# A two-layer block and a three-branch block on one core: a place for each weights' unit inside a longer slot, and a ring with one slot less

## The chip, the cores and the metric

The kernel runs on one core of a Trainium2 chip. The metric is the device time of one execution in microseconds, lower is better. Everything is computed in 32-bit floating point as far as the reader of the output can see; inside, TensorE multiplies in fp32r, a 32-bit format of which the kernel makes two parts for each number (below).

## The reference, cut to what matters

A sequence of 256 tokens with 1024 features goes through two layers, an even one and an odd one, and then through a second block with another set of weights. Norms are RMS norms over 1024 features.

```python
for layer in range(2):                      # first_block
    y = rms_norm(h, nw[0])
    y = even_mixer(y, ...) if layer % 2 == 0 else odd_mixer(y, ...)
    h = h + rms_norm(y, nw[1])
    y = conv_ffn(rms_norm(h, nw[2]), ffn_w_up[layer], conv_w, conv_b, ffn_w_down[layer])
    h = h + rms_norm(y, nw[3])
# even_mixer: proj = y @ w_in; window attention with rope and sinks, beside a gated
#             recurrence in blocks of 32 tokens (HGRN2); concat @ w_out
# odd_mixer:  proj = y @ w_in; attention in chunks of 64 with a relative bias; @ w_out
# conv_ffn:   up = y @ w_up (1024 x 5632); gelu(conv3(u)) * v; @ w_down (2816 x 1024)
# second block: proj = y @ w_in_2; three attentions (block-sparse, with forget gates, over a
#             memory of 256 rows); each @ its branch matrix, gated and summed; @ w_out_2;
#             then a gated feed-forward of the same size as above
```

Nearly all of the arithmetic is in the products of 256 tokens with weights that are read once from memory.

## The kernel before

**Units and slots.** The weights come as 347 units, at most 128 partitions by 1024 numbers each, in the order in which TensorE uses them (`STREAM`: even_a, even_f, even_q, even_i, fill, even_out, lead0, up0, down0, odd_v, odd_qk, odd_out, lead1, up1, down1, moba_qk, both_v, fox_qk, mem_q, forget, gates, branches, merge_out, lead2, up2, down2). For each unit three things are kept in SBUF: the raw numbers, the high part (the raw numbers rounded to fp32r) and the low part (raw minus high). They stand in slots: `raw` and `hi` are tensors of `RAW` = 10 slots of 1024 numbers, and `lo` takes the same addresses as `raw`, since the split overwrites in place. `ring()` says which slot a unit takes and which earlier unit, its giver, must have been used before; up to the end of fill only `FEW` = 8 slots are in the ring, because the last two hold the memory's normed rows (`m_hi`, `m_lo`) until then.

**One unit's way.** SP issues the load (L500) after it has waited until TensorE has used the giver (`unit_used`). ACT waits for the load and rounds (L593, `round_unit`), DVE waits for ACT and subtracts (L1483, `split_unit`), and TensorE waits for DVE (`lo_done`). The orders of ACT's and DVE's work are written out by hand: a call `units(upto)` between other work says up to which unit they shall have gone on.

```python
act.activation(hi[:, s, :w], raw[:, s, :w], ACT.Copy).then_inc(hi_done, 1)
...
dve.tensor_tensor(lo[:, s, :w], raw[:, s, :w], hi[:, s, :w].bitcast(F32), ALU.subtract).then_inc(lo_done, 1)
```

**Three products.** The tokens are kept in a high and a low part as well (`y_hi` and `y_lo`, the two halves of `y_both`; `h_hi` and `h_lo` for the feed-forward's inner features). A product of tokens and weights is the sum of high by high, high by low and low by high. Where tokens are the stationary operand (`tokens_unit`, L927: even_a, odd_v, down, merge_out and others; the same pattern at L1142, L1157, L1190, L1283 and L1344), the moving operand is 512 or 256 columns of a weights' part. Where weights are stationary, the moving operand is the tokens: `features_of` (L1008) moves 256 columns three times, `features_pair` (L1017 and L1018, the units of up) moves `y_both`, 512 columns, against the high part and `y_hi`, 256 columns, against the low part.

**Changes of stage.** Before even_out, down, odd_out and merge_out end, the last `TAIL` = 7 units are gone through for the first tile of 128 tokens and then for the second (`by_tile`), so that the first tile's norm runs while TensorE works on the second. The next stage begins with `LEAD` = 6 units gone through in the same way. Between the two lies a norm (on ACT, DVE and POOL), the turning of the normed rows by TensorE (L1029, `turn`), and the making of y_hi on ACT and y_lo on DVE. `norms_between` on ACT, and a like function on DVE, say how many units are prepared between the parts of the norm:

```python
units(last(name) + RAW - TAIL)
square_product(g, 0, base, tile_done, TAILS.index(name) + 1)
square_sum(g + 1, 0, p)
units(last(name) + 4)
turned_hi(stage, turn_base, y_hi, (0,))
units(last(name) + 5)
```

`BIAS_AT`, the points in the stream at which SP loads the odd layer's bias, counts from `RAW` too.

Of the kernel before, what the change touches and what calls it, by code (L numbers as in the profile page):

```python
# [44 lines left out]
UNIT = 1024  # L45
RAW = 10

# [15 lines left out]
UNITS = len(WIDTH)  # L63
FEW = 8

# [22 lines left out]

SLOT, GIVER, TURN = ring()
TAILS = ["even_out", "down0", "odd_out", "down1", "merge_out", "down2"]  # L90

# [113 lines left out]
def build(nc, dram, out):  # L205
    with ExitStack() as ctx:
# [237 lines left out]
        def token_half(y, kh, t):  # L444

            return y[:, 4 * kh:4 * kh + 4, t * P:(t + 1) * P]

        @block.sync
        def _(sp):
# [463 lines left out]
        def _(pe):  # L913
# [3 lines left out]
            def tokens_unit(name, n, t, base, y, splits, lo_last=False, y_lo_at=None):  # L917

                yh, yl = y
                k, tok = n - FIRST[name], slice(t * P, (t + 1) * P)  # L920
                for i, (x, w) in enumerate(((yh, hi), (yl, hi), (yh, lo)) if lo_last else ((yh, hi), (yh, lo), (yl, hi))):
                    if i == 2 and lo_last:
# [3 lines left out]
                    for half_, (c0, cw) in enumerate(splits):  # L926
                        mm = pe.matmul(ps[:, base + 2 * t + half_, :cw], x[:, k, tok], w[:, SLOT[n], c0:c0 + cw],  # L927
                                       start=i == 0 and k == 0, stop=i == 2 and n == last(name) - 1)
                return mm

            def last_unit(y):

                n, k = UNITS - 1, COUNT["down2"] - 1
                for c in range(2):
                    for x, w in ((y[0], hi), (y[0], lo), (y[1], hi)):
                        mm = pe.matmul(ps[:, 6 + c, :], x[:, k, P:S], w[:, SLOT[n], 512 * c:512 * c + 512],
                                       start=False, stop=x is y[1])
# [57 lines left out]

            def features_of(n, s, outs, y, nk=KD, cols=P, stage=None):

# [4 lines left out]
                for f, dst in enumerate(outs):  # L1002
                    for k in range(nk):
                        if stage is not None and k % 4 == 0:
                            pe.wait_ge(y_lo_done, 4 * stage + 3 + k // 4)
                        at = slice(k * cols + f * P, k * cols + (f + 1) * P)
                        for w, x, first, final in ((hi, yh, True, False), (hi, yl, False, False), (lo, yh, False, True)):
                            mm = pe.matmul(dst, w[:, s, at], x(k), start=first and k == 0, stop=final and k == nk - 1)  # L1008
# [110 lines left out]
            for f in range(4):  # L1119
                n = FIRST["even_f"] + f  # L1120
                features_of(n, SLOT[n], [ps[:, f // 2, (f % 2) * S:(f % 2 + 1) * S]], of_tiles(Y)).then_inc(unit_used, 1)
            for f in range(4):
# [4 lines left out]
                n = FIRST["even_q"] + f  # L1127
                features_of(n, SLOT[n], [ps[:, 2 + f // 2, (f % 2) * S:(f % 2 + 1) * S]], of_tiles(Y)).then_inc(unit_used, 1)
            pe.wait_ge(qf_evac, 2)
# [6 lines left out]
            for n in range(FIRST["even_i"], last("even_i")):  # L1136
                wait_unit(n)
                for t in range(NT):
                    for kk in range(2):
                        k = 2 * (n - FIRST["even_i"]) + kk  # L1140
                        for x, w in ((y_hi, hi), (y_hi, lo), (y_lo, hi)):
                            mm = pe.matmul(ps[:, 4 + t, :], x[:, k, t * P:(t + 1) * P], w[:, SLOT[n], 512 * kk:512 * kk + 512],  # L1142
                                           start=k == 0 and x is y_hi and w is hi, stop=k == KD - 1 and x is y_lo)
                mm.then_inc(unit_used, 1)

            def fill(first, a, b):

                for i, k in ((first + step // KD, step % KD) for step in range(a, b)):
# [5 lines left out]
                    if t == 0 and k % 4 == 0:  # L1154
                        wait_unit(n)
                    for x, w in ((yh, hi), (yh, lo), (yl, hi)):
                        mm = pe.matmul(ps[:, 6, t * 256:t * 256 + 256], x[:, k, t * P:(t + 1) * P], w[:, SLOT[n], c],  # L1157
                                       start=k == 0 and x is yh and w is hi, stop=k == KD - 1 and x is yl)
                    if t == 1 and k % 4 == 3:
# [24 lines left out]
            def even_part(u, t):  # L1184
                n, k, tok = FIRST["even_out"] + u, (u + 4) % 8, slice(t * P, (t + 1) * P)
                if t == 0:
                    wait_unit(n)
                for x, w in ((y_hi, hi), (y_hi, lo), (y_lo, hi)):
                    for c in range(2):
                        mm = pe.matmul(ps[:, (0, 6)[t] + c, :], x[:, k, tok], w[:, SLOT[n], 512 * c:512 * c + 512],  # L1190
                                       start=u == 0 and x is y_hi and w is hi, stop=u == KD - 1 and x is y_lo)
                if t == 1:
# [65 lines left out]
            def feed_forward(layer, stage, base, turn_next=lambda: None):  # L1258
# [3 lines left out]
                def lead(t):  # L1262
                    tok = slice(t * P, (t + 1) * P)
                    for j in range(LEADS):
                        for half_ in range(2):
# [7 lines left out]
                            if j == 0:  # L1273
                                pe.wait_ge(y_hi_done, 4 * stage + 2 * t + half_ + 1)
                            order = ((y_hi, hi), (y_lo, hi), (y_hi, lo)) if last_lead else ((y_hi, hi), (y_hi, lo), (y_lo, hi))
                            for i, (x, w) in enumerate(order):
# [4 lines left out]
                                for kk in range(4):  # L1281
                                    k, c = 4 * half_ + kk, slice(256 * kk, 256 * kk + 256)
                                    mm = pe.matmul(lead_place(layer, j, t), x[:, k, tok], w[:, SLOT[n], c],  # L1283
                                                   start=k == 0 and i == 0, stop=k == KD - 1 and i == 2)
# [41 lines left out]
            def qk_half(j, f):  # L1326
# [3 lines left out]
                if j >= 2:  # L1330
                    pe.wait_ge((q_evac, k_evac)[f], j - 1)
                features_of(n, SLOT[n], [qk_place(j, f)], of_tiles(Y)).then_inc(unit_used, 1)

# [4 lines left out]
            def out_part(k, t):  # L1338
                n, tok = FIRST["odd_out"] + k, slice(t * P, (t + 1) * P)
                if t == 0:  # L1340
                    wait_unit(n)
                for x, w in ((0, hi), (0, lo), (1, hi)):
                    for c in range(2):
                        mm = pe.matmul(ps[:, (6, 0)[t] + c, :], out_y(x, k // 4, tok)[:, k % 4, :], w[:, SLOT[n], 512 * c:512 * c + 512],  # L1344
                                       start=k == 0 and x == 0 and w is hi, stop=k == KD - 1 and x == 1)
                if t == 1:
# [55 lines left out]
            def gate_unit(u):  # L1402
                if u >= 2:
                    pe.wait_ge(gate_evac, u - 1)
                for f in range(2):
                    n = FIRST["gates"] + 2 * u + f
                    features_of(n, SLOT[n], [ps[:, 6 + u % 2, f * S:(f + 1) * S]], of_tiles(Y)).then_inc(unit_used, 1)

            pe.wait_ge(v2_evac, 2)
            n = FIRST["forget"]  # L1410
            features_of(n, SLOT[n], [ps[:, 1, 0:S]], of_tiles(Y)).then_inc(unit_used, 1)
            pe.wait_ge(c_evac, 2)
# [42 lines left out]
            for u in range(6):  # L1455
# [11 lines left out]
                for i in range(2):  # L1467
                    n = FIRST["branches"] + 2 * u + i
                    outs = [ps[:, 2 * (u % 2) + i, f * S:(f + 1) * S] for f in range(2)]
                    features_of(n, SLOT[n], outs, ys, 4, 256).then_inc(unit_used, 1)  # L1470
            tokens_by("merge_out", 4, (h_hi, h_lo), needs=lambda u: (merged_lo, u // 4 + 1),
# [508 lines left out]
```

## Time and profile before

| what | value |
|---|---|
| median of 3 runs | 1099.36 us (1096.43 to 1099.52) |
| the profiled execution: its own time, and its span | 1095.97 us, 1094.2 us |
| TensorE busy with matmuls | 1086.5 us, 99%, 6712 instructions |
| weight loads | 959.7 us, 88% |
| DVE | 746.0 us, 68% |
| ACT | 600.1 us, 55% |
| POOL | 112.4 us, 10% |
| DMA | 192.81 MB, mean 176 GB/s; weights' queue 54.1% of 16 engines' span |

The span is that of the instructions on the core; the time has what lies around it as well. Matmuls are pipelined and overlap in the record, so the duration that a row gives for one of them is longer than the time from its start to the next one's start.

### The profile page before, as it was taken

To read this page: it belongs to the slowest core of one execution; us is meant where nothing else is said; L and a number is where in the kernel's file an instruction comes from. 1 tells how busy PE (TensorE), PEld (TensorE's weight loads), DVE (VectorE), ACT (ScalarE), POOL (GpSimd) and SP (SyncE) were. 2 spreads that over 40 slices of the span, in tenths; PEclk is the share of its full clock that TensorE was granted. 3 is DMA by queue.
4 is the path that set the end of the run, shared out by engine and by line. 5 is a ranking of instruction groups with operands and counts; after the bars stand their busy time and mean duration, and the time that the engine had idled before them with its cause. 6 is when DMAs were issued, how large, how long until landed. Compare 5 with 4: busy or idle time off the path is not lost.

```text
span 1094.2 us, 16724 instructions
## 1 busy us (share of the span) xinstructions
PE 1086.5 (99%) x6712; PEld 959.7 (88%) x6712; DVE 746.0 (68%) x1107; ACT 600.1 (55%) x994; POOL 112.4 (10%) x129
## 2 busy tenths in 40 slices
PE   8999999999999999999999999999999999999998
PEld 7988989888888899898888888889999989888887
DVE  6876595998846566859788566766656885666651
ACT  5744465776734545557667445357444644555640
POOL 5020000121100000001111001121000000111100
PEclk9999999999999999999999999999999999999999
DMA  8851366665664754366656656464333545565661
GB/s 304 286 174 59 121 206 213 193 189 190 182 193 152 269 150 149 124 225 188 188 190 183 194 183 211 136 234 134 115 99 113 165 160 196 190 182 185 191 194 39
DMA packets 56957, 192.81 MB, mean 176 GB/s; under 512 B 6704, under 2 KB 9648, under 8 KB 56880
## 3 DMA queue, kind: packets, MB, share of 16 engines
q1 hardware_dynamic: 56880, 191.74, 54.1%
q8 instruction: 53, 0.87, 0.3%
q14 instruction: 24, 0.20, 0.1%
HBM read 190.67 MB, written 1.05 MB: 175 GB/s over the span
## 4 chain that ended last, share of the span: by engine, by line
PE 94%; DVE 3%; POOL 1%; issue 1%; ACT 1%; DMA 0%; SPq 0%; DVEq 0%; ACTq 0%
PE ps L927 28%; PE ps L1017 19%; PE ps L1008 15%; PE ps L1018 10%; PE ps L1283 5%; PE ps L1157 3%; PE ps L1103 3%; PE ps L1080 2%; PE ps L1344 2%; DVE lo L1483 1%; PE ps L1092 1%; PE ps L1029 1%; PE ps L1142 1%; POOL hr L538 1%; PE ps L1049 1%; PE ps L1167 1%
## 5 line engine op out<-in xcount | busy, mean ns | idle before, releaser
L1483 DVE TENSOR_TENSOR lo<-raw,hi 128x1024 fp32r<-128x1024 f32 (+2 forms) x347 | 429.0, 1263 | 81.0 <-ACT hi L593 78.3
L593 ACT ACTIVATE hi<-raw 128x1024 fp32r<-128x1024 f32 (+2 forms) x347 | 347.3, 1037 | 84.3 <-DMA raw<-in_weights 77.6
L1017 PE MATMUL ps<-y_both,hi 128*128 128x512 f32 x912 | 320.8, 397 | 0.0
L1018 PE MATMUL ps<-y_both,lo 128*128 128x256 f32 x912 | 255.0, 280 | 0.0
L1017 PEld LDWEIGHTS ps<-y_both,hi 128*128 128x128 f32 x912 | 171.3, 188 | 41.5
L1018 PEld LDWEIGHTS ps<-y_both,lo 128*128 128x128 f32 x912 | 172.0, 189 | 0.0
L1008 PE MATMUL ps<-y_both,hi 128*128 128x256 f32 x912 | 167.6, 285 | 0.4 <-DVE lo L1483 0.4
L1008 PEld LDWEIGHTS ps<-y_both,hi 128*128 128x128 f32 x912 | 141.8, 191 | 1.1 <-DVE lo L1483 0.6
L1008 PE MATMUL ps<-y_both,lo 128*128 128x256 f32 x456 | 128.9, 283 | 0.0
L927 PE MATMUL ps<-hi,y_both 128*128 128x512 f32 x352 | 93.9, 381 | 1.1 <-DVE lo L1483 1.0
L927 PE MATMUL ps<-hi,h_hi 128*128 128x512 f32 x294 | 90.9, 391 | 0.0
L927 PE MATMUL ps<-lo,h_hi 128*128 128x512 f32 x294 | 90.6, 389 | 0.0
L927 PE MATMUL ps<-hi,h_lo 128*128 128x512 f32 x294 | 90.6, 389 | 0.0
L1008 PEld LDWEIGHTS ps<-y_both,lo 128*128 128x128 f32 x456 | 87.2, 191 | 0.0
L547 POOL TENSOR_TENSOR h_lo<-pt,h_hi 128x256 fp32r<-128x256 f32 x66 | 51.4, 779 | 324.0 <-ACT h_hi L663 324.0
L1650 DVE TENSOR_TENSOR pr<-ps,pr 128x512 f32<-128x512 f32 x57 | 39.3, 689 | 57.7 <-ACT pr L677 57.7
L677 ACT ACTIVATE pr<-ps 128x512 f32<-128x512 f32 x57 | 33.9, 595 | 79.1 <-PE ps L1018 79.1
L927 PEld LDWEIGHTS ps<-hi,y_both 128*128 128x128 f32 x352 | 63.6, 188 | 14.5 <-DVE lo L1483 1.6
L927 PEld LDWEIGHTS ps<-hi,h_lo 128*128 128x128 f32 x294 | 55.2, 188 | 11.6
L927 PEld LDWEIGHTS ps<-lo,h_hi 128*128 128x128 f32 x294 | 55.2, 188 | 11.5
L927 PEld LDWEIGHTS ps<-hi,h_hi 128*128 128x128 f32 x294 | 54.7, 188 | 11.0
L653 ACT ACTIVATE pr<-sc,neg 128x128 f32<-128x128 f32 x80 | 35.5, 446 | 51.5 <-DVE neg L1616 51.4
(288 smaller groups left out, 1386.4 us busy)
## 6 DMA issues: line engine op xcount, KB each, us to landing
raw<-in_weights SPq DMA_DIRECT2D x331, 512.0 KB, 3.7
gain<-in_gains SPq DMA_DIRECT2D x11, 512.0 KB, 7.1
raw<-in_weights SPq DMA_DIRECT2D x8, 384.0 KB, 7.1
bias<-in_rel SPq DMA_DIRECT2D x16, 128.0 KB, 2.1
raw<-in_weights SPq DMA_DIRECT2D x8, 256.0 KB, 2.6
mem_x<-in_mem SPq DMA_DIRECT2D x2, 512.0 KB, 10.9
h<-in_x SPq DMA_DIRECT2D x2, 256.0 KB, 3.9
h<-in_x SPq DMA_DIRECT2D x1, 512.0 KB, 6.1
```

The source lines that it names most:

```text
L547: pool.tensor_tensor(h_lo[:, j, :], pt[:, j % 2, :S], h_hi[:, j, :].bitcast(F32), ALU.subtract).then_inc(h_lo_done, 1)
L593: act.activation(hi[:, s, :w], raw[:, s, :w], ACT.Copy).then_inc(hi_done, 1)
L653: e = act.activation(pr[:, a % 2, c], src, ACT.Exp, bias=neg[:, col, t:t + 1], accum_out=tot[:, col, t:t + 1])
L677: act.activation(pr[:, j % 2, :].rearrange("p (a b) -> p a b", a=2), both_parts(j, 1), ACT.Copy).then_inc(low_part, 1)
L927: mm = pe.matmul(ps[:, base + 2 * t + half_, :cw], x[:, k, tok], w[:, SLOT[n], c0:c0 + cw], start=i == 0 and k == 0, stop=i == 2 and n == ...
L1008: mm = pe.matmul(dst, w[:, s, at], x(k), start=first and k == 0, stop=final and k == nk - 1)
L1017: pe.matmul(dst, hi[:, s, at], y_both[:, :, k, :], start=k == 0, stop=False)
L1018: mm = pe.matmul(dst[:, 0:S], lo[:, s, at], y_hi[:, k, :], start=False, stop=k == KD - 1)
L1103: mm = pe.matmul(place(stage, hh, t), pt[:, a % 2, i * P:(i + 1) * P], v(kt), start=kt == 0, stop=kt == kts[-1])
L1283: mm = pe.matmul(lead_place(layer, j, t), x[:, k, tok], w[:, SLOT[n], c], start=k == 0 and i == 0, stop=k == KD - 1 and i == 2)
L1483: dve.tensor_tensor(lo[:, s, :w], raw[:, s, :w], hi[:, s, :w].bitcast(F32), ALU.subtract).then_inc(lo_done, 1)
L1650: dve.tensor_tensor(p, both_parts(j, 0), p, ALU.add).then_inc(summed, 1)
```

## The change

The ring has nine slots instead of ten, and seven instead of eight until the end of fill. Each slot is longer by 112 numbers (448 bytes), and a unit begins in its slot at a place of its own: the high part at one of eight steps of 64 bytes, the raw numbers and the low part, which share their memory, at another one of eight. `places()` counts the units of each of six kinds of use (`KIND`: 0 tokens stationary, 1 `features_of`, 2 up, 3 lead, 4 branches, 5 fill) and gives the i-th of a kind the place 27·i mod 64, of which the remainder by eight is the high part's step and the quotient the low part's. The 64 places of a kind thus come up in turn. Every tensor that is allocated behind the slots lies 128 bytes lower than before. The memory's normed rows become lists of slots, since their two slots are no longer next to each other without a gap. Everything that counts from `RAW` or `FEW` shifts by one. The instructions and their order per engine are otherwise the same.

The diff, cut (the same replacement of `hi[:, SLOT[n], ...]` by `at_hi(n)[:, ...]`, and of `lo` by `at_lo(n)`, is made in `last_unit`, `features_of`, even_i, `fill`, even_out, lead and odd_out as well):

```diff
-RAW = 10
+RAW = 9
...
-FEW = 8
+FEW = 7
...
+KIND = {"even_f": 1, "even_q": 1, "odd_qk": 1, "forget": 1, "gates": 1, "up0": 2, "up1": 2, "up2": 2, "lead0": 3, "lead1": 3, "lead2": 3,
+        "branches": 4, "fill": 5}
+def places():
+
+    seen, out = [0] * 6, []
+    for name, n, _, _ in STREAM:
+        kind = KIND.get(name, 0)
+        for _ in range(n):
+            i = 27 * seen[kind] % 64
+            out.append((16 * (i % 8), 16 * (i // 8)))
+            seen[kind] += 1
+    return out
+
+
+PLACE = places()
...
-            lo = sb("lo", [RAW, UNIT], F32R, r)
-        raw = sb("raw", [RAW, UNIT])
-        hi = sb("hi", [RAW, UNIT], F32R)
+            lo = sb("lo", [RAW, UNIT + 112], F32R, r)
+        raw = sb("raw", [RAW, UNIT + 112])
+        hi = sb("hi", [RAW, UNIT + 112], F32R)
...
-        m_hi = lo[:, FEW:RAW, :].rearrange("p a (b s) -> p (a b) s", s=S)
-        m_lo = hi[:, FEW:RAW, :].rearrange("p a (b s) -> p (a b) s", s=S)
+        m_hi = [lo[:, a, :UNIT].rearrange("p (b s) -> p b s", s=S) for a in range(FEW, RAW)]
+        m_lo = [hi[:, a, :UNIT].rearrange("p (b s) -> p b s", s=S) for a in range(FEW, RAW)]
+
+        def at_hi(n):
+            return hi[:, SLOT[n], PLACE[n][0]:PLACE[n][0] + UNIT]
+
+        def at_lo(n):
+            return lo[:, SLOT[n], PLACE[n][1]:PLACE[n][1] + UNIT]
+
+        def at_raw(n):
+            return raw[:, SLOT[n], PLACE[n][1]:PLACE[n][1] + UNIT]
...
+            if type(y) is list:
+                return y[kh][:, :, t * P:(t + 1) * P]
...
-                sp.dma_start(raw[:, SLOT[n], :WIDTH[n]], dram["weights"][n][:, :WIDTH[n]]).then_inc(raw_in[SLOT[n]], 16)
+                sp.dma_start(at_raw(n)[:, :WIDTH[n]], dram["weights"][n][:, :WIDTH[n]]).then_inc(raw_in[SLOT[n]], 16)
...
-                act.activation(hi[:, s, :w], raw[:, s, :w], ACT.Copy).then_inc(hi_done, 1)
+                act.activation(at_hi(n)[:, :w], at_raw(n)[:, :w], ACT.Copy).then_inc(hi_done, 1)
...
-                for i, (x, w) in enumerate(((yh, hi), (yl, hi), (yh, lo)) if lo_last else ((yh, hi), (yh, lo), (yl, hi))):
+                for i, (x, w) in enumerate(((yh, at_hi), (yl, at_hi), (yh, at_lo)) if lo_last else ((yh, at_hi), (yh, at_lo), (yl, at_hi))):
                     if i == 2 and lo_last:
                         wait_unit(n)
                     if i == 2 and y_lo_at is not None:
                         pe.wait_ge(y_lo_done, y_lo_at)
                     for half_, (c0, cw) in enumerate(splits):
-                        mm = pe.matmul(ps[:, base + 2 * t + half_, :cw], x[:, k, tok], w[:, SLOT[n], c0:c0 + cw],
+                        mm = pe.matmul(ps[:, base + 2 * t + half_, :cw], x[:, k, tok], w(n)[:, c0:c0 + cw],
...
-                s = SLOT[n]
                 pe.wait_ge(lo_done, n + 1)
                 for k in range(KD):
                     at = slice(k * P, (k + 1) * P)
-                    pe.matmul(dst, hi[:, s, at], y_both[:, :, k, :], start=k == 0, stop=False)
-                    mm = pe.matmul(dst[:, 0:S], lo[:, s, at], y_hi[:, k, :], start=False, stop=k == KD - 1)
+                    pe.matmul(dst, at_hi(n)[:, at], y_both[:, :, k, :], start=k == 0, stop=False)
+                    mm = pe.matmul(dst[:, 0:S], at_lo(n)[:, at], y_hi[:, k, :], start=False, stop=k == KD - 1)
...
-                s, w = SLOT[n], WIDTH[n]
+                w = WIDTH[n]
...
-                dve.tensor_tensor(lo[:, s, :w], raw[:, s, :w], hi[:, s, :w].bitcast(F32), ALU.subtract).then_inc(lo_done, 1)
+                dve.tensor_tensor(at_lo(n)[:, :w], at_raw(n)[:, :w], at_hi(n)[:, :w].bitcast(F32), ALU.subtract).then_inc(lo_done, 1)
```

## Rows read from the trace of the kernel before

**Rows 1.** Page, first part: busy us, share of the span and instructions of each engine.

```profile
span 1094.2 us, 16724 instructions
...
PE 1086.5 (99%) x6712; PEld 959.7 (88%) x6712; DVE 746.0 (68%) x1107; ACT 600.1 (55%) x994; POOL 112.4 (10%) x129
```

**Rows 2.** Waits of TensorE, whole span: us in total, times, longest us.

```profile
PE ps L927 <- DVE lo L1483: 1.0, 2, 0.6
PE ps L1008 <- DVE lo L1483: 0.4, 1, 0.4
```

**Rows 3.** Chain that ended last, whole span: start us, us, what.

```profile
286.02 57.15 PE ps L927 x252
...
852.69 28.79 PE ps L1008 x240
```

**Rows 4.** Groups by shape, TensorE: xcount | busy us, mean ns | idle before.

```profile
L1017 PE MATMUL ps<-y_both,hi 128*128 128x512 f32 x912 | 320.8, 397 | 0.0
...
L936 PE MATMUL ps<-hi,h_lo 128*128 128x512 f32 x2 | 0.8, 388 | 0.0
```

**Rows 5.** Timeline of TensorE, up of layers 0 and 1: start us, us, what.

```profile
200.05 0.40 PE L1017 MATMUL ps<-y_both,hi 128*128 128x512 f32 x1
...
209.76 0.40 PE L1017 MATMUL ps<-y_both,hi 128*128 128x512 f32 x1
...
519.97 0.40 PE L1017 MATMUL ps<-y_both,hi 128*128 128x512 f32 x1
...
529.86 0.40 PE L1017 MATMUL ps<-y_both,hi 128*128 128x512 f32 x1
```

**Rows 6.** Groups by shape, TensorE, the attentions' products.

```profile
L1103 PE MATMUL ps<-v,pt 128*128 128x64 f32 x192 | 24.6, 278 | 0.0
...
L1103 PE MATMUL ps<-mv,pt 128*128 128x128 f32 x32 | 3.9, 275 | 0.0
```

**Rows 7.** Timeline of ACT, first stage; in brackets idle time before, and releaser.

```profile
28.17 1.06 ACT L593 ACTIVATE hi<-raw 128x1024 fp32r<-128x1024 f32 x1 [2.03 <-DMA raw<-in_weights]
29.14 2.55 ACT L721 ACTIVATE xhat<-xhat,rstd 128x512 f32<-128x512 f32 x4
31.59 1.04 ACT L593 ACTIVATE hi<-raw 128x1024 fp32r<-128x1024 f32 x1
```

**Rows 8.** Timeline of DVE, first stage.

```profile
29.26 1.23 DVE L1483 TENSOR_TENSOR lo<-raw,hi 128x1024 fp32r<-128x1024 f32 x1 [1.09 <-ACT hi L593]
```

**Rows 9.** Timeline of TensorE, first stage: the first matmuls of even_f.

```profile
29.71 0.40 PE L1008 MATMUL ps<-y_both,hi 128*128 128x256 f32 x2
```

**Rows 10.** Waits of SP's DMA queue: us in total, times, longest us.

```profile
SPq L500 <- PE ps L1018: 283.0, 114, 3.8
```

**Rows 11.** Page, DMA issues: xcount, KB each, us to landing.

```profile
raw<-in_weights SPq DMA_DIRECT2D x331, 512.0 KB, 3.7
```

**Rows 12.** Timeline of DVE, from down0 to odd_v.

```profile
343.28 1.22 DVE L1483 TENSOR_TENSOR lo<-raw,hi 128x1024 fp32r<-128x1024 f32 x1
344.41 1.28 DVE L1527 TENSOR_TENSOR y_both<-ps,y_both 128x512 fp32r<-128x512 f32 x2
...
346.93 1.47 DVE L1507 TENSOR_TENSOR xhat<-ps,gain 128x512 f32<-128x512 f32 x2
...
352.90 0.88 DVE L1521 TENSOR_SCALAR xhat<-xhat,rstd 128x512 f32<-128x512 f32 x2 [0.66 <-POOL rstd L532]
```

**Rows 13.** Timeline of TensorE, from down0 to odd_v.

```profile
347.63 1.07 PE L927 MATMUL ps<-hi,y_both 128*128 128x512 f32 x4
...
353.54 1.06 PE L1029 MATMUL ps<-ident,xhat 128*128 128x128 f32 x8
```

**Rows 14.** Timeline of DVE, from merge_out to lead2.

```profile
907.64 0.88 DVE L1521 TENSOR_SCALAR xhat<-xhat,rstd 128x512 f32<-128x512 f32 x2 [0.67 <-POOL rstd L532]
```

**Rows 15.** Timeline of TensorE, from merge_out to lead2.

```profile
911.18 1.04 PE L1029 MATMUL ps<-ident,xhat 128*128 128x128 f32 x8
```

More of the change, by code:

```diff
@@ L934, in last_unit @@
                 for c in range(2):
-                    for x, w in ((y[0], hi), (y[0], lo), (y[1], hi)):
-                        mm = pe.matmul(ps[:, 6 + c, :], x[:, k, P:S], w[:, SLOT[n], 512 * c:512 * c + 512],
+                    for x, w in ((y[0], at_hi), (y[0], at_lo), (y[1], at_hi)):
+                        mm = pe.matmul(ps[:, 6 + c, :], x[:, k, P:S], w(n)[:, 512 * c:512 * c + 512],
                                        start=False, stop=x is y[1])
@@ L994, in tokens_by, with features_of @@
                     by_tile(n, TAIL, False, True)
-            def features_of(n, s, outs, y, nk=KD, cols=P, stage=None):
+            def features_of(n, outs, y, nk=KD, cols=P, stage=None):
                 pe.wait_ge(lo_done, n + 1)
@@ L1006, in features_of @@
                         at = slice(k * cols + f * P, k * cols + (f + 1) * P)
-                        for w, x, first, final in ((hi, yh, True, False), (hi, yl, False, False), (lo, yh, False, True)):
-                            mm = pe.matmul(dst, w[:, s, at], x(k), start=first and k == 0, stop=final and k == nk - 1)
+                        for w, x, first, final in ((at_hi, yh, True, False), (at_hi, yl, False, False), (at_lo, yh, False, True)):
+                            mm = pe.matmul(dst, w(n)[:, at], x(k), start=first and k == 0, stop=final and k == nk - 1)
                 return mm
             def features_pair(n, dst):
-                s = SLOT[n]
                 pe.wait_ge(lo_done, n + 1)
@@ L1120, in _ @@
                 n = FIRST["even_f"] + f
-                features_of(n, SLOT[n], [ps[:, f // 2, (f % 2) * S:(f % 2 + 1) * S]], of_tiles(Y)).then_inc(unit_used, 1)
+                features_of(n, [ps[:, f // 2, (f % 2) * S:(f % 2 + 1) * S]], of_tiles(Y)).then_inc(unit_used, 1)
             for f in range(4):
@@ L1127, in _ @@
                 n = FIRST["even_q"] + f
-                features_of(n, SLOT[n], [ps[:, 2 + f // 2, (f % 2) * S:(f % 2 + 1) * S]], of_tiles(Y)).then_inc(unit_used, 1)
+                features_of(n, [ps[:, 2 + f // 2, (f % 2) * S:(f % 2 + 1) * S]], of_tiles(Y)).then_inc(unit_used, 1)
             pe.wait_ge(qf_evac, 2)
@@ L1140, in _ @@
                         k = 2 * (n - FIRST["even_i"]) + kk
-                        for x, w in ((y_hi, hi), (y_hi, lo), (y_lo, hi)):
-                            mm = pe.matmul(ps[:, 4 + t, :], x[:, k, t * P:(t + 1) * P], w[:, SLOT[n], 512 * kk:512 * kk + 512],
-                                           start=k == 0 and x is y_hi and w is hi, stop=k == KD - 1 and x is y_lo)
+                        for x, w in ((y_hi, at_hi), (y_hi, at_lo), (y_lo, at_hi)):
+                            mm = pe.matmul(ps[:, 4 + t, :], x[:, k, t * P:(t + 1) * P], w(n)[:, 512 * kk:512 * kk + 512],
+                                           start=k == 0 and x is y_hi and w is at_hi, stop=k == KD - 1 and x is y_lo)
                 mm.then_inc(unit_used, 1)
@@ L1155, in fill @@
                         wait_unit(n)
-                    for x, w in ((yh, hi), (yh, lo), (yl, hi)):
-                        mm = pe.matmul(ps[:, 6, t * 256:t * 256 + 256], x[:, k, t * P:(t + 1) * P], w[:, SLOT[n], c],
-                                       start=k == 0 and x is yh and w is hi, stop=k == KD - 1 and x is yl)
+                    for x, w in ((yh, at_hi), (yh, at_lo), (yl, at_hi)):
+                        mm = pe.matmul(ps[:, 6, t * 256:t * 256 + 256], token_half(x, k // 4, t)[:, k % 4, :], w(n)[:, c],
+                                       start=k == 0 and x is yh and w is at_hi, stop=k == KD - 1 and x is yl)
                     if t == 1 and k % 4 == 3:
@@ L1187, in even_part @@
                     wait_unit(n)
-                for x, w in ((y_hi, hi), (y_hi, lo), (y_lo, hi)):
+                for x, w in ((y_hi, at_hi), (y_hi, at_lo), (y_lo, at_hi)):
                     for c in range(2):
-                        mm = pe.matmul(ps[:, (0, 6)[t] + c, :], x[:, k, tok], w[:, SLOT[n], 512 * c:512 * c + 512],
-                                       start=u == 0 and x is y_hi and w is hi, stop=u == KD - 1 and x is y_lo)
+                        mm = pe.matmul(ps[:, (0, 6)[t] + c, :], x[:, k, tok], w(n)[:, 512 * c:512 * c + 512],
+                                       start=u == 0 and x is y_hi and w is at_hi, stop=u == KD - 1 and x is y_lo)
                 if t == 1:
@@ L1274, in lead @@
                                 pe.wait_ge(y_hi_done, 4 * stage + 2 * t + half_ + 1)
-                            order = ((y_hi, hi), (y_lo, hi), (y_hi, lo)) if last_lead else ((y_hi, hi), (y_hi, lo), (y_lo, hi))
+                            order = ((y_hi, at_hi), (y_lo, at_hi), (y_hi, at_lo)) if last_lead else ((y_hi, at_hi), (y_hi, at_lo), (y_lo, at_hi))
                             for i, (x, w) in enumerate(order):
@@ L1282, in lead @@
                                     k, c = 4 * half_ + kk, slice(256 * kk, 256 * kk + 256)
-                                    mm = pe.matmul(lead_place(layer, j, t), x[:, k, tok], w[:, SLOT[n], c],
+                                    mm = pe.matmul(lead_place(layer, j, t), x[:, k, tok], w(n)[:, c],
                                                    start=k == 0 and i == 0, stop=k == KD - 1 and i == 2)
@@ L1331, in qk_half @@
                     pe.wait_ge((q_evac, k_evac)[f], j - 1)
-                features_of(n, SLOT[n], [qk_place(j, f)], of_tiles(Y)).then_inc(unit_used, 1)
+                features_of(n, [qk_place(j, f)], of_tiles(Y)).then_inc(unit_used, 1)
             def turn_out(kh, t):
@@ L1341, in out_part @@
                     wait_unit(n)
-                for x, w in ((0, hi), (0, lo), (1, hi)):
+                for x, w in ((0, at_hi), (0, at_lo), (1, at_hi)):
                     for c in range(2):
-                        mm = pe.matmul(ps[:, (6, 0)[t] + c, :], out_y(x, k // 4, tok)[:, k % 4, :], w[:, SLOT[n], 512 * c:512 * c + 512],
-                                       start=k == 0 and x == 0 and w is hi, stop=k == KD - 1 and x == 1)
+                        mm = pe.matmul(ps[:, (6, 0)[t] + c, :], out_y(x, k // 4, tok)[:, k % 4, :], w(n)[:, 512 * c:512 * c + 512],
+                                       start=k == 0 and x == 0 and w is at_hi, stop=k == KD - 1 and x == 1)
                 if t == 1:
@@ L1406, in gate_unit @@
                     n = FIRST["gates"] + 2 * u + f
-                    features_of(n, SLOT[n], [ps[:, 6 + u % 2, f * S:(f + 1) * S]], of_tiles(Y)).then_inc(unit_used, 1)
+                    features_of(n, [ps[:, 6 + u % 2, f * S:(f + 1) * S]], of_tiles(Y)).then_inc(unit_used, 1)
             pe.wait_ge(v2_evac, 2)
             n = FIRST["forget"]
-            features_of(n, SLOT[n], [ps[:, 1, 0:S]], of_tiles(Y)).then_inc(unit_used, 1)
+            features_of(n, [ps[:, 1, 0:S]], of_tiles(Y)).then_inc(unit_used, 1)
             pe.wait_ge(c_evac, 2)
@@ L1469, in _ @@
                     outs = [ps[:, 2 * (u % 2) + i, f * S:(f + 1) * S] for f in range(2)]
-                    features_of(n, SLOT[n], outs, ys, 4, 256).then_inc(unit_used, 1)
+                    features_of(n, outs, ys, 4, 256).then_inc(unit_used, 1)
             tokens_by("merge_out", 4, (h_hi, h_lo), needs=lambda u: (merged_lo, u // 4 + 1),
```

## Prediction

> **What bounds the kernel now.** The page's first part comes first: TensorE has a matmul in it for 1086.5 us of a span of 1094.2 [rows 1]. That alone says little, since matmuls overlap in the record, so the second view is the table of waits: in the whole span TensorE's matmuls wait 1.4 us for the low parts of the weights, in three waits [rows 2]. DMA, ACT and DVE therefore set the time only where they make TensorE late. The third view is the chain of work: it runs through TensorE for hundreds of matmuls at a stretch, and length over count gives the price of one. 252 matmuls of 512 columns take 57.15 us, 226.8 ns each; 240 of 256 columns take 28.79 us, 120.0 ns each [rows 3]. The granted clock is full in every slice of the page, the level of 2.4 GHz, at which 512 columns are 213.3 ns and 256 are 106.7. So each matmul costs 13.4 ns above its columns, whatever its width. The listing by shape counts 33 groups of matmuls with the parts of the weights (the largest and the smallest are shown), 5,664 matmuls in all [rows 4]; at 13.4 ns that is 76 us. The change moves the operands of just these matmuls, so this is the only place from which much could come.
>
> **Term 1, the new places.** No instruction is added or removed: the same 347 loads, 347 roundings on ACT and 347 splits on DVE, and the same matmuls, with other addresses. Before, every weights' part starts at the same distance from a multiple of 512 bytes as y and h do; afterwards the high and the low part of a unit stand at any of eight distances from them. Does TensorE's time depend on that? Two things in the trace bear on it. In the units of up a matmul of 512 columns and one of 256 alternate; the same code, with the same distances, settles into two rhythms. In layer 0 the first of 29 such pairs starts at 200.05 and the last at 209.76; in layer 1 at 519.97 and 529.86 [rows 5]. Over 28 steps that is 346.8 and 353.2 ns a pair: 6.4 ns apart, 3.2 ns a matmul. So a matmul's cost can differ with nothing but timing, and something between weight loads and moving reads does interfere a little. Against dependence on the place: the attention's products with v, of which every other head reads v 256 bytes further on, last 278 ns on the mean, and 275 those with mv, all at one distance [rows 6]. That is 3 ns at most, but these matmuls are narrow.
> Nothing in this trace shows a wide matmul at another distance, so the cost is bounded from both sides: down to minus 76 us (all that stands above the columns gone); up to 5,664 × 3.2 = 18 us if the slower rhythm's surplus came everywhere, and 36 us if it came twice. I take 0: 226.8 and 120.0 have the same surplus in stages whose operands lie quite differently in the memory, and a constant fits that better than collisions do.
> The Trainium skill (TensorE: Matmul & The Clock Gate, "Step-by-step: what each phase is for") says that the weight load and the moving operand have read ports of their own and that the one takes no bandwidth from the other. By that rule the term is 0 as well; the two rhythms are not what it leads one to expect.
>
> **Term 2, the first stage, with seven slots.** With eight slots the eight units of even_a are all loaded at once. With seven, the last of them, and each later unit, takes the place of the next one in SP's queue, behind the wait for a slot. So each rounding starts where the next unit's did: unit 8's at 28.17, where unit 9's was, and unit 9's at 31.59, where unit 10's was [rows 7]. A unit is ready about 2.3 us after its rounding starts (29.26 + 1.23 − 28.17 [rows 7, 8]). Unit 8 is then ready at 28.2 + 2.3 = 30.5, a little less because unit 7, which now goes ahead, is shorter: 30.3. TensorE comes to it at 29.71 [rows 9]: 0.6 late. Unit 9 is ready at 31.6 + 2.3 = 33.9 and wanted 24 matmuls of 120 ns later, at 30.3 + 2.9 = 33.2: 0.7 late. ACT has 2.55 us of the memory's norm in its queue after unit 9 [rows 7], so unit 10 starts at 31.6 + 1.04 + 2.55 = 35.2 and is ready at 37.5, wanted at 33.9 + 2.9 = 36.8: 0.7 late. From unit 11 on the loads run ahead again. Sum 2.0 us; bounds 0.5 (if the landings move less than one place) and 3 (if DVE's rotary work makes unit 12 late too).
>
> **Term 3, the ring of nine, at the changes of stage.** In a long stage it is SP that waits for slots: 114 times in up alone, 283.0 us [rows 10], while TensorE waits for almost no unit. There a slot less takes 8 × 353 = 2.8 us from a lead nine units long, some 25 us, of which landing takes 3.7 [rows 11] and rounding and split 2.3. Nothing happens. It is at the tails that it counts: seven units are held until the second token tile has passed. The count of units that ACT and DVE prepare before the norm, RAW − TAIL, falls from 3 to 2; the third is now done between the first tile's norm and its y, on DVE ahead of y_lo. Take down0 to odd_v: DVE splits a unit at 343.28, makes y_lo at 344.41, splits another, and begins the second tile's norm at 346.93 [rows 12]. One split more in that row (1.13 us from start to start, 343.28 to 344.41) moves the norm's start to 348.06, since its input is ready earlier and DVE is what it waits for; the scaled row comes at 354.03 instead of 352.90. TensorE turns it at 353.54, with the first half ready at 352.90 + 0.44, so 0.2 us is spare [rows 12, 13]: 0.9 to 1.0 us late. y_lo of the first tile, at 345.54 to 346.8, is still in time for the matmul at 347.63 [rows 13]. Queued behind the late norm are odd_v's second tile and everything after it; nothing later gives the time back, because TensorE waits nowhere else. The same order of work stands at even_out to lead0, odd_out to lead1 and down1 to moba_qk: four times 1.0 = 4.0 us. At merge_out to lead2 DVE has scaled by 908.5 and TensorE turns at 911.18 [rows 14, 15]: 2.7 us to spare, no cost. Bounds: 0 if the additional split finds a gap, 6 if the third unit also lands late (it waits for a slot that is freed one place later, 6 × 226.8 ns = 1.36 us) and holds up ACT's y_hi.
>
> DVE's and ACT's reads and DMA's writes at steps of 64 bytes I cost at nothing: their work on weights lies under TensorE's by the lead of term 3, and 10% on a split would be 0.12 us. Where that cover is thin, at the four changes of stage, it would add half a microsecond in all.
>
> **Sum.** 0 + 2.0 + 4.0 = 6.0 us on the profiled execution's 1095.97 us gives 1102.0; that execution is 3.4 us under the median of the runs shown (1099.36), two of which lie at 1099.4 and one at 1096.4. Between 1102.0 and 1105.4 I name **1104.0 us**. A difference under 0.3%, 3.3 us, can't be told from none.
>
> **Rivals.**
> A, faster: the surplus is a collision between weight load and moving read that comes from equal distances, and most new places avoid it. For it: the surplus is the same for 512 and 256 columns, like a cost per weight load; the two rhythms show that something there gives way. Against: [rows 6], and the same surplus where the operands differ. It decides from 6.0 us / 5,664 = 1.1 ns saved on the mean matmul. With 3.3 ns it is 18.7 us: 1104 − 18.7 = 1085; with half the surplus, 6.7 ns, 38 us: 1066. The skill (the same page, "Wait — 56ns, not 53.3ns?") has only 2.5 ns above the columns for a warm matmul; by it about 11 ns × 5,664 = 62 us would be there to get, an estimate, and the time 1042. This trace doesn't agree: 13.4 ns.
> B, slower: equal distances are the good case (weight load and moving read start together and never cross), and mixed ones collide. Price 3.2 ns a matmul, 18 us, to twice that: 1122 to 1140. For it: the slower rhythm exists; against: nothing shows that place brings it on.
> C, no difference that can be told: places are indifferent, and the ring's loss is covered, or layers 1 and 2 fall into the quicker rhythm, which is 2 × 304 pairs × 6.4 ns = 3.9 us: 1099 to 1102. The places then change nothing.
>
> **How the numbers follow.** Forecast (places indifferent, ring paid for, 1102.7 to 1109): 0.36. B: 0.26. A: 0.20. C: 0.18. Slower by over 0.3%: 0.36 + 0.26 = 0.62; within: 0.18; faster: 0.20. The range leaves out about half of A's cases (below 1074) and the dearer third of B's (above 1126); the forecast's own range is 1102.7 to 1109.
>
> **What would show it.** The chain's price per matmul in down (226.8) and in branches (120.0), unit by unit: constant, and term 1 is right; spread over values in the same stage, and A or B is. A wait of matmuls on the low parts of about 2 us between 29 and 38 us: term 2. Turning matmuls that wait on DVE's scaled rows by about 1 us at four changes of stage, none at lead2: term 3. If wide matmuls change by more than 1.1 ns on the mean, the forecast is wrong by its first term, and the ring's terms matter little.

## The result and the profile after

The changed kernel takes 1111.04 us (median of 4 runs, 1110.40 to 1111.51), the kernel before 1097.89 us over its 4 runs: a ratio of 1.0124, 95% interval 1.0106 to 1.0142. It is 13.2 us slower, where 4.6 us were forecast. The profiled execution took 1110.93 us, 15.0 more than that of before.

The page of the changed kernel, its first part, to set against [rows 1]:

```profile
span 1109.1 us, 16723 instructions
...
PE 1090.8 (98%) x6712; PEld 958.9 (86%) x6712; DVE 745.9 (67%) x1107; ACT 600.5 (54%) x994; POOL 110.0 (10%) x129
```

The span has grown by 14.9 us, TensorE's busy time by 4.3 only. So most of it is waiting. The waits of TensorE's matmuls in the changed kernel (us in total, times, longest), to set against [rows 2]:

```profile
PE ps L1054 <- DVE xhat L1546: 5.9, 5, 2.3
PE ps L1369 <- DVE y_both L1827: 5.6, 1, 5.6
PE ps L1034 <- DVE lo L1508: 1.7, 3, 0.8
...
PE ps L953 <- DVE lo L1508: 0.2, 1, 0.2
```

The turning's row before, which [rows 2] does not have:

```profile
PE ps L1029 <- DVE xhat L1521: 1.8, 2, 1.5
```

L1054 is the turning of normed rows (L1029 before), the wait of term 3, and 1.8 of its 5.9 us were there before; L1034 is the features' wait for low parts, that of term 2. L1369, a single wait of 5.6 us in odd_out, stands in no step of the prediction.

**Where the time went.** Both traces hold 6,712 matmul records in the same order. Each interval from one start to the next can therefore be set against the same interval before. Intervals that differ by more than 60 ns are waits come or gone; the sum of all the others is a change of price. In us, against the profiled execution of before (the runs are told below):

| where | changed | run 1 | run 2 | run 3 | run 4 | run 5 | run 6 | run 7 | run 8 |
|---|---|---|---|---|---|---|---|---|---|
| before the first product with weights | 1.8 | 2.1 | -0.6 | 2.4 | 2.3 | 0.8 | 1.8 | 2.5 | 2.0 |
| first stage (term 2) | 0.9 | 0.6 | 2.1 | 2.0 | 0.4 | 0.0 | 2.0 | 2.6 | -0.9 |
| even_out to lead0 | 0.3 | 0.9 | 0.6 | 0.8 | 0.1 | -0.2 | 0.4 | 2.7 | 0.1 |
| down0 to odd_v | 1.9 | 1.6 | 1.5 | 1.1 | 1.1 | 0.0 | 1.1 | 2.9 | 1.0 |
| odd_out | 7.3 | 0.0 | 7.9 | 8.3 | 7.4 | 0.0 | 0.0 | 0.0 | 0.0 |
| odd_out to lead1 | 1.3 | 1.2 | 1.4 | 1.6 | 1.2 | 0.0 | 1.4 | 4.1 | 0.6 |
| down1 to moba_qk | 1.7 | 0.7 | 1.5 | 1.1 | 1.5 | 0.0 | 2.0 | 4.5 | 0.9 |
| price of matmuls | -0.1 | -0.2 | 2.2 | -19.6 | 10.5 | -3.3 | -19.6 | -20.1 | 0.4 |

At merge_out to lead2 it is 0.0 in all of them; intervals elsewhere, up to 0.8 us in sum, are left out. The first row is the start, in which TensorE waits for the tokens and the first gains; it differs by about 3 us between runs, in run 8 by 2.0 with the addresses and the first loads of before, so it is taken for scatter. Without it the changed kernel's column gives 0.9 + 0.3 + 1.9 + 7.3 + 1.3 + 1.7 - 0.1 = 13.3, where 13.2 were measured; beside a scatter of that size, the agreement to 0.1 us is luck.

**The wait in odd_out.** The chain of the changed kernel there (start us, us, what):

```profile
454.24 3.63 DMA raw<-in_weights
457.86 0.02 issue
457.89 1.06 ACT hi L619
458.94 0.49 ACT y_both L823
459.44 0.02 issue
459.46 0.70 DVE y_both L1827
```

and ACT's timeline (in brackets the idle time before, and the releaser):

```profile
445.95 2.94 ACT L619 ACTIVATE hi<-raw 128x1024 fp32r<-128x1024 f32 x3
457.89 1.06 ACT L619 ACTIVATE hi<-raw 128x1024 fp32r<-128x1024 f32 x1 [9.00 <-DMA raw<-in_weights]
458.85 1.07 ACT L823 ACTIVATE y_both<-ps 128x512 fp32r<-128x512 f32 x2
```

Four units stand in ACT's queue ahead of the high parts of odd_out's second half of rows (L823): `units(last("odd_out") + 2)`, a count that the change leaves alone. The fourth is the second unit of lead1. With ten slots it took the slot of odd_qk's last unit, long free. With nine it takes the slot of odd_out's first unit, and that is held until the second token tile has passed it. So ACT stands for 9.0 us in front of a load which waits for TensorE, while the rows that TensorE needs next lie behind it in ACT's queue. TensorE has other work up to 454.6, then none. The wait costs more than its own length, as the windows show (us, busy of PE, PEld, DVE, ACT and POOL, granted clock, DMA share, GB/s):

```profile
448.00:454.00 6.00, 6.00 (x37) 5.17 (x36) 4.70 (x7) 0.88 (x1) 0.00 (x0) 1.00 0.01 3
454.00:460.00 6.00, 0.64 (x5) 0.36 (x3) 0.54 (x1) 2.03 (x3) 0.00 (x0) 0.72 0.28 87
460.00:463.00 3.00, 2.79 (x7) 2.21 (x8) 3.00 (x4) 0.00 (x0) 0.00 (x0) 0.50 0.00 0
463.00:469.00 6.00, 6.00 (x27) 4.89 (x26) 1.39 (x3) 1.30 (x4) 0.00 (x0) 0.96 0.00 0
```

After some 5.6 us without work the granted clock is 0.50, the level of 1.2 GHz, in the 3 us in which the work resumes. From start to start, the interval with the wait in it is 5.8 us longer than before, and the eight behind it are 1.5 us longer together: 7.3 us in all.

**The change from down0 to odd_v.** The chain of the changed kernel:

```profile
343.33 5.19 DMA raw<-in_weights
348.52 0.02 issue
348.54 1.07 ACT hi L619
349.61 0.02 issue
349.63 1.23 DVE lo L1508
350.86 1.20 DVE y_both L1552 x2
352.06 1.13 DVE lo L1508
353.19 0.61 DVE xhat L1532
...
359.08 0.50 DVE xhat L1546
359.58 0.14 issue
359.72 1.06 PE ps L1054 x8
```

It is term 3's order, read backwards: the turning waits for the scaled rows, these for the norm's start, that for two splits around y_lo. But at its head stands a load, with 5.19 us from issue to landing: the bound of the prediction in which the third unit also lands late. Such a load stands at the head at odd_out to lead1 and at down1 to moba_qk too, and not at even_out to lead0, the change of stage that lost only 0.3 us.

**The price.** Two pieces of the changed kernel's chain stand where [rows 3] stood, branches, and down2 for a stage like down0:

```profile
868.54 27.99 PE ps L1034 x240
...
1045.00 59.54 PE ps L953 x258
```

That is 116.6 ns a matmul of 256 columns (120.0 before) and 230.8 ns a matmul of 512 (226.8). Both have moved by over 3 ns, in opposite directions. Here are the means above the columns at 2.4 GHz, in ns, by kind of use (from start to start between matmuls with weights, steps over 40 ns above the columns left out; the mean of a unit, then of the units):

| kind | matmuls | before | changed | run 3 | run 4 | run 6 |
|---|---|---|---|---|---|---|
| tokens stationary | 1,617 | 13.8 | 17.6 | 13.9 | 19.8 | 13.9 |
| features | 1,119 | 13.1 | 11.2 | 7.5 | 13.0 | 7.4 |
| up | 1,817 | 15.6 | 14.4 | 10.1 | 16.6 | 10.1 |
| lead | 426 | 13.2 | 11.3 | 10.7 | 12.5 | 10.6 |
| branches | 285 | 13.2 | 10.0 | 6.8 | 11.8 | 6.8 |
| fill | 250 | 12.5 | 11.7 | 10.2 | 12.1 | 10.1 |

In the changed kernel the tokens' kind costs 1,617 × 3.8 = 6.1 us more; the others give back 2.1, 2.2, 0.8, 0.9 and 0.2 us, together 6.2. The sum is nothing, and neither part of it is. Unit by unit the price spreads from 6.7 to 20 ns, and much of the spread goes with the two distances: tokens at 3 and 3 steps cost 19.6, 19.8 and 20.0 ns, at 7 and 3 they cost 19.3, 20.0 and 20.2, at 0 and 0 twice 14.6. Not all of it does: tokens at 5 and 6 cost 13.6, 18.5 and 20.1, and of four units of up at 1 and 4, three cost 10.0 to 10.1 and one 15.0. The spread alone is therefore a hint; runs 3 and 4 below are the test. A distance is counted from y or h, in steps of 64 bytes modulo 512, that of the high part first.

### The profile page after: what moved, and what is told of

It is laid out like the page before. It is cut to its first block, busy times and chain, and to the rows that moved or that the text cites. A ratio compares the mean times of both kernels' runs of the same rounds, so it can differ in the third digit from the quotient of the medians.

```text
span 1109.1 us, 16723 instructions
## 1 busy us (share of the span) xinstructions
PE 1090.8 (98%) x6712; PEld 958.9 (86%) x6712; DVE 745.9 (67%) x1107; ACT 600.5 (54%) x994; POOL 110.0 (10%) x129
## 4 chain that ended last, share of the span: by engine, by line
PE 87%; DVE 5%; DMA 3%; POOL 2%; ACT 1%; issue 1%; SPq 1%; DVEq 0%; ACTq 0%
PE ps L953 25%; PE ps L1042 19%; PE ps L1034 14%; PE ps L1043 10%; PE ps L1308 3%; PE ps L1182 3%; PE ps L1128 3%; DMA raw<-in_weights 3%; PE ps L1105 2%; DVE lo L1508 2%; PE ps L1369 2%; PE ps L1117 1%; PE ps L1167 1%; PE ps L1054 1%; POOL hr L564 1%
## 5 line engine op out<-in xcount | busy, mean ns | idle before, releaser
L1034 PE MATMUL ps<-y_both,hi 128*128 128x256 f32 x912 | 165.4, 284 | 1.7 <-DVE lo L1508 1.7
L1034 PEld LDWEIGHTS ps<-y_both,hi 128*128 128x128 f32 x912 | 139.7, 189 | 2.9 <-DVE lo L1508 2.3
L1034 PE MATMUL ps<-y_both,lo 128*128 128x256 f32 x456 | 127.9, 280 | 0.0
L1034 PEld LDWEIGHTS ps<-y_both,lo 128*128 128x128 f32 x456 | 86.1, 189 | 0.0
L953 PEld LDWEIGHTS ps<-hi,h_hi 128*128 128x128 f32 x294 | 54.7, 188 | 12.1
## 6 DMA issues: line engine op xcount, KB each, us to landing
mem_x<-in_mem SPq DMA_DIRECT2D x2, 512.0 KB, 10.4
```

What stands on the lines that cost most here:

```text
L1034: mm = pe.matmul(dst, w(n)[:, at], x(k), start=first and k == 0, stop=final and k == nk - 1)
```

## The experiments

Times are medians; the ratio is to the kernel before on the same chip (1098.33 us beside runs 1 to 4, 1097.6 beside the others).

**Run 1: the order in odd_out.** On ACT, in the changed kernel:

```diff
-            units(last("odd_out") + 2)
+            units(last("odd_out") + 1)
             out_hi(1, 0)
```

> The changed kernel, with ACT rounding one unit less ahead of the turned rows of odd_out. Theory 'order' (the 5.6 us wait and the cold matmuls behind it come from a rounding queued ahead of work on which the slot it waits for depends): the wait goes, some 7 us less, about 1104 us. Rival 'late loads' (the units' loads themselves have become slower at places of 64 bytes): nothing changes, 1111 us.

Measured 1102.89 us, ratio 1.0039 (1.0027 to 1.0052). The wait at L1369 is gone, and 8.2 us with it. The loads are as they were, 4.3 us to landing at the median and 4.2 in the changed kernel: 'order' holds, 'late loads' falls.

**Run 2: the ring alone.** In the kernel before:

```diff
-RAW = 10
+RAW = 9
...
-FEW = 8
+FEW = 7
```

> The kernel before with nine slots (seven at first) of 1024 numbers, every part at the old distance. Theory 'waits make it all, places sum to nothing': the same waits as in the changed kernel, about 1111 us, and the price of a matmul constant as before. Rival 'places cost': less than half of the 13 us, 1098 to 1104 us.

Measured 1109.92 us, ratio 1.0093 (1.0069 to 1.0118). The profiled execution, 1112.52 us, has the changed kernel's waits, and its chain has the prices of before:

```profile
869.25 28.79 PE ps L1008 x240
...
1047.57 58.54 PE ps L927 x258
```

The 2.2 us in its last row of the table are the two rhythms: layer 0's up now runs in the slower one. Its timeline has 28 pairs from 199.76 to 209.66, 353.6 ns each, in place of 346.8 [rows 5]:

```profile
199.76 0.40 PE L1017 MATMUL ps<-y_both,hi 128*128 128x512 f32 x1
...
209.66 0.40 PE L1017 MATMUL ps<-y_both,hi 128*128 128x512 f32 x1
```

So the ring makes most of the loss, nearly all of it by waits; the slower rhythm is the rest.

**Run 3: one good pair of distances for each kind.** In the changed kernel, `places()` chooses by kind:

```diff
+WANT = ((0, 0), (1, 7), (3, 0), (3, 1), (1, 7), (3, 7))
...
-            i = 27 * seen[kind] % 64
-            out.append((16 * (i % 8), 16 * (i // 8)))
+        wh, wl = WANT[KIND.get(name, 0)]
+        out.append((16 * ((wh - 1 - 71 * SLOT[n]) % 8), 16 * ((wl - 2 - 71 * SLOT[n]) % 8)))
```

(A slot of 4,544 bytes begins 71 steps after the one before it, so the same distance is another place in each slot.)

> The changed kernel, but each kind of use has one fixed pair of distances from y instead of 64: tokens stationary 0 and 0, features 1 and 7 steps of 64 bytes, up 3 and 0, lead 3 and 1, branches 1 and 7, fill 3 and 7. Theory 'the price of a matmul depends on the two distances, and the survey's mean hides it': features at 6.7 ns above the columns, up at 10, tokens at 13.6, some 20 us less, 1091 us. Rival 'constant surplus, the spread is noise': 1111 us.

Measured 1092.93 us, ratio 0.9946 (0.9926 to 0.9966), 18 us under the changed kernel with all its waits still there. Branches and down2 in its chain:

```profile
857.02 27.22 PE ps L1033 x240
...
1029.41 58.51 PE ps L952 x258
```

113.4 ns and 226.8 ns. 'Constant surplus' falls.

**Run 4: one dear pair for each kind.** As run 3, with

```diff
+WANT = ((7, 3), (0, 0), (4, 4), (2, 3), (6, 1), (6, 7))
```

> The changed kernel with the dearest pair of distances for each kind: tokens 7 and 3, features 0 and 0, up 4 and 4, lead 2 and 3, branches 6 and 1, fill 6 and 7. Theory 'distances set the price': tokens 19.8 ns, features 12.9, up 16.9, about 11 us more, 1122 us. Rival 'constant surplus': 1111 us.

Measured 1120.31 us, ratio 1.0201 (1.0181 to 1.0221).

```profile
875.08 28.48 PE ps L1033 x240
...
1053.53 60.20 PE ps L952 x258
```

233.3 ns in down2. 'Constant surplus' falls here too. An obvious rival is that the other engines and the DMA disturb TensorE's reads, since the places move their accesses as well. Two windows of 8 us in down2 speak against it (columns as above), one with them at work and one behind the last load, rounding and split:

```profile
1088.00:1096.00 8.00, 8.00 (x36) 6.42 (x35) 3.62 (x3) 3.02 (x3) 0.00 (x0) 1.00 0.41 131
1097.00:1105.00 8.00, 8.00 (x36) 6.42 (x35) 0.00 (x0) 0.00 (x0) 0.00 (x0) 1.00 0.01 2
```

From start to start a matmul takes 233.3 ns in both; in run 3 it is 226.7 on either side of the last split. Places alone move this kernel over 27 us, from 1092.9 to 1120.3, with the same instructions in the same order.

**Run 5: ten slots and two pads.** In the kernel before:

```diff
+        sb("pad_hi", [96])
         hi = sb("hi", [RAW, UNIT], F32R)
+        sb("pad_y", [16])
...
-        sb("align", [96])
+        sb("align", [64])
```

> The kernel before, ten slots, with pads only: every high part 7 steps of 64 bytes and every low part 1 step behind y (modulo 512), the feed-forward's inner features 6 steps from y. Theory 'distances set the price, the ring does the rest': features 6.7 ns above the columns, up 13.5, tokens about 15.8, in sum some 11 us less than before: 1087 us, with no new waits. Rival 'constant surplus': 1098 us.

Measured 1093.11 us, ratio 0.9951 (0.9936 to 0.9966). Faster than before, with no wait added, but by 4.5 us and not by 11. Features came to 10.4 ns on the mean, and they have two levels at these distances, 6.7 and 12.2. The chain shows both, even_f with even_q, and branches:

```profile
30.83 14.26 PE ps L1010 x120
...
852.73 27.25 PE ps L1010 x240
```

118.8 ns against 113.5 (of the branches, one in three takes its tokens from h_hi, at other distances). Within odd_qk and gates, whose weights all stand at the same distances, single units cost 6.6 to 7.7 or 12.2 to 12.5 ns. Up has two levels too: 28 pairs take 9.71 us in layer 0 and 9.90 us in layer 1, 346.8 and 353.6 ns:

```profile
199.66 0.39 PE L1019 MATMUL ps<-y_both,hi 128*128 128x512 f32 x1
...
209.37 0.39 PE L1019 MATMUL ps<-y_both,hi 128*128 128x512 f32 x1
...
519.91 0.40 PE L1019 MATMUL ps<-y_both,hi 128*128 128x512 f32 x1
...
529.81 0.40 PE L1019 MATMUL ps<-y_both,hi 128*128 128x512 f32 x1
```

A unit's price in the spread of the changed kernel is therefore no safe forecast for a long stretch at the same distances. Tokens came out dearer as well, 16.7 ns for 15.8.

**Run 6: runs 1 and 3 together.**

> The fixed pairs of distances of the third run together with the order of the first. If the two effects simply add: 1092.9 less 8 is 1085 us. If one hides the other: 1089 us or more.

Measured 1084.75 us, ratio 0.9876 (0.9858 to 0.9893). The two effects add, and this is faster than both kernels, by 13 us and by 26.

**Run 7: one unit fewer ahead of the second norm.** In run 6's kernel, on ACT and DVE:

```diff
-                units(last(name) + 4)
+                units(last(name) + 3)
...
-                units(last(name) + 5)
+                units(last(name) + 4)
```

> As the run before it, and at each change of stage ACT and DVE prepare one unit less ahead of the second tile's norm, the unit being made up behind it. Theory 'the split ahead of the norm on DVE is what the turning waits for': four waits of 1.2 to 1.9 us go, 5 us less, 1080 us. Rival 'the units land late there': no gain, 1085 us.

Measured 1096.07 us, ratio 0.9989 (0.9971 to 1.0006): 11 us worse than run 6, so both theories missed. The turning waits less (3.0 us), but what was put off is what the next stage's lead asks for:

```profile
PE ps L952 <- DVE lo L1507: 5.7, 4, 2.7
PE ps L1307 <- DVE lo L1507: 5.0, 2, 2.5
PE ps L1053 <- DVE xhat L1545: 3.0, 2, 2.8
```

**Run 8: the order of nine slots with ten.** In the kernel before, on ACT and DVE:

```diff
-                units(last(name) + RAW - TAIL)
+                units(last(name) + RAW - TAIL - 1)
```

> The kernel before, ten slots, in which ACT and DVE prepare two units instead of three before the first tile's norm, as with nine slots, so that the third stands between the norm and y. Theory 'order on DVE alone': the turning of the second tile waits about 1 us more at four changes of stage, 1102 us. Rival 'the late landing of a unit makes it': 1098 us.

Measured 1100.27 us, ratio 1.0023 (1.0012 to 1.0034). That lies between the two theories. At the four changes of stage it adds 0.1 + 1.0 + 0.6 + 0.9 = 2.6 us, and in its chain no load stands ahead of any of the four turnings. The changed kernel has 5.0 there, with a load in the chain at three of them. Order makes about half; the later landing is left for the rest, which no run has tested by itself.

**Run 9: the third split in DVE's idle gap.** In run 6's kernel, DVE makes one unit less ahead of y_lo and makes it up while it waits for POOL's root:

```diff
-                units(last(name) + 4)
+                units(last(name) + 3)
                 turned_lo(stage, turn_base, y_lo, y_hi, (0,))
-                units(last(name) + 5)
+                units(last(name) + 4)
                 weigh_product(g, 1, base, unit_used, last(name))
-                add_product(g, p, 1)
+                add_product(g, p, 1, lambda: units(last(name) + 5))
```

> The sixth run's kernel, with DVE's third split at each change of stage moved from ahead of y_lo into the gap in which DVE waits for POOL's root in the second tile's norm. Theory 'the split delays the norm, and DVE has 0.7 us of idle time there': the turning waits some 0.5 us less at each of four changes, 1083 us. Rival 'a unit becomes late instead, as in the seventh run': 1086 us or more.

Measured 1085.83 us, ratio 0.9892 (0.9874 to 0.9911): no different from run 6. The turning waits 7.4 us in six waits, in run 6 it was 6.2 in five. Inconclusive between the theories: nothing was won, and no low part became late either.

**Run 10: everything 64 bytes further on.** In run 6's kernel:

```diff
+        sb("pad", [16])
         with ExitStack() as r:
             lo = sb("lo", [RAW, UNIT + 112], F32R, r)
```

> The sixth run's kernel with 64 bytes more ahead of everything, so that all distances between operands stay and all addresses move. Theory 'distances count, not addresses': 1085 us and the same prices by kind. Rival 'addresses modulo 512 count': tokens or features change by 3 ns or more, 5 us or more either way.

Measured 1085.35 us, ratio 0.9889 (0.9869 to 0.9909). All kinds within 0.2 ns of run 6. With this one shift of 64 bytes, the price goes with the distance between operands and not with the address.

## Why the prediction was right and wrong

The direction was right, and the measured 1111 lies in the range; the size was not, 4.6 us forecast and 13.2 measured. The step that failed is in term 3: "It is at the tails that it counts", followed by four changes of stage. Only the counts that depend on `RAW` were looked at. The fifth place is a count that does not depend on it, ACT's `units(last("odd_out") + 2)`: it was right for ten slots, and with nine it asks for a unit whose slot is still held. The prediction has no term for odd_out at all and gives no reason for leaving it out. The wait and the lower clock behind it cost 7.3 us there, and run 1, which changes nothing but this order, takes them away with nine slots in place.

**Term 1**, taken as 0, came out at -0.1 us by luck, for the wrong reason. "A constant fits that better than collisions do" is refuted by runs 3 and 4: whole kinds move between 6.8 and 11.8 ns (branches) or 13.9 and 19.8 (tokens) with the distances. The evidence could not have decided it: the two stages compared, at 226.8 and 120.0 ns, both stand at equal distances. The sum is 0 because the tokens' kind, cheap at equal distances (13.8 ns, and 17.6 on the mean of the places), lost what the other kinds won. Rivals A and B were both at work, each in some of the stages. That the same code has two rhythms was the sign, and it was read as a matter of timing alone. The upper bound of 3.2 ns on every matmul held for the whole (18 us at most, and 10.5 in run 4), but not for each kind: the tokens' kind rose by 3.8 ns in the changed kernel and by 6.0 in run 4, near twice 3.2. The Trainium skill (TensorE: Matmul & The Clock Gate, "Step-by-step: what each phase is for") says that weight load and moving operand have read ports of their own and that the load takes no bandwidth from the running matmul. Taken alone this gives no reason for a distance to matter, yet one matmul shape took 113.4 ns (run 3) and 120.0 (before); whether the ports are where the distance acts, no run shows.

**Term 2**, 2.0 us: 0.9 in the changed kernel's trace, 0.4 to 2.6 in the runs with seven slots at first. Right in place. Its size goes with the start: in run 8, which has eight slots at first and starts about as late (2.0 us against 1.8), this stage is 0.9 us shorter than before, so beside a like start the seven slots cost 1.8. It also goes with the price: 2.0 and more where the features are cheap (runs 3, 6 and 7), 0.4 where they are dear (run 4). That the loads set the pace there would explain both; no run tests it.

**Term 3**, 4.0 us at four changes of stage and none at lead2: 5.0 (0.3 + 1.9 + 1.3 + 1.7, rounded) and 0.0. The mechanism was right. Order is half of it (run 8, 2.6 us), less than the 4.0 put down for it; with the unit that also lands late, the bound of 6, the measured 5.0 lies midway.

Rival C's quicker rhythm in layers 1 and 2 did not come; run 2 lost it in layer 0 instead.

Open stays why a distance costs what it does, and what decides between two levels at the same distances. Distances to the weight load and to the next moving read were not separated. Ten slots with a pair of distances for each kind were not tried: they need 20 x (4,544 - 4,096) = 8,960 bytes more of each partition than the kernel before.

## What to carry to other kernels

When a ring shrinks, look up in each engine's written order every count of units, also those that name no ring size, and ask for each which slot it wants and who still holds it: an in-order queue that waits for a load, with the releaser's own input behind it, stands still. A mean over a spread of variants can hide two effects of opposite sign; sort by kind of use before calling a parameter indifferent. When matmuls show a constant surplus above their columns, try the distance between their operands modulo 512 bytes for each kind of use, and time it over a long stretch, since a single unit does not show the settled rhythm.

## What the runs showed of the hardware

The surplus of a wide fp32r matmul above its columns goes with the distance in SBUF between stationary and moving operand, and hardly with the address (run 10, one shift of 64 bytes, means by kind within 0.2 ns). Multiples of 512 bytes made no difference: in run 3 the units of both_v and fox_qk stand in all nine slots and every one costs 13.3 ns. Over long stretches at one pair of distances the surplus was 6.7 ns for branches at 1 and 7 steps (run 3), 13.5 for down2 at 0 and 0 (run 3's chain) and 20.0 at 7 and 3 (run 4's), 10.1 for up at 3 and 0 (run 3). The same pair can hold two levels, 6.7 and 12.2 for features at 7 and 1 in run 5. After about 5.6 us without matmuls the granted clock was 0.50 in the next 3 us, and the eight intervals from start to start in that time were 1.5 us longer.
